# Expert results scattered to token order and read back by plain loads; the first expert's rows prepared in halves

## The chip, the cores and the metric

One core of a Trainium2 chip runs the whole program. The metric is the device time of one execution in microseconds (us). The kernel before takes 1114.15 us, the median of 3 runs (1113.95 to 1116.16).

## The reference, cut to what matters

The program computes two layers of a network over 512 tokens of 1024 numbers each, in float32, and a final RMSNorm. Each layer ends in a mixture of experts (MoE), and the change is there and in what follows it:

```python
def moe_route(flat, router_w, router_b):          # flat: (512, 1024)
    s = sigmoid(flat @ router_w)                  # 16 experts in 4 groups
    biased = s + router_b
    grp_score = sum(top_k(biased per group, 2))   # best group ...
    g_sel = argmax(grp_score)
    idx = top_k(where(in_group, biased, -inf), 2) # ... and the best two experts in it
    w = take(s, idx); w = w / sum(w)
    return combine                                # (512, 16), two weights per token

out = 0
for e in range(16):
    hid = silu(flat @ w_gate[e]) * (flat @ w_up[e])      # 1024 -> 512
    out = out + combine[:, e:e + 1] * (hid @ w_down[e])  # 512 -> 1024
```

After layer 0's MoE comes layer 1's pooling mixer (a norm, four banded averages over neighbouring tokens, four 256x256 products), after layer 1's MoE the final norm. With the reference's inputs the experts get these numbers of tokens: layer 0: 29 46 25 40 87 70 86 61 87 91 82 106 56 62 62 34; layer 1: 31 35 18 26 89 73 76 60 84 87 77 118 51 68 74 57.

## The kernel before

**One expert after the other, 128 rows at a time.** The tokens lie in SBUF as 4 tiles of 128 (`x`). Their normed, modulated rows are also in HBM (`xh_dram`, "xh_scratch" in the profile). From the router's choice DVE and TensorE make, for each expert, a list of its token numbers (`lists`, 128 x 16; places without a token hold 0, so token 0's row is fetched for them). GpSimd fetches an expert's 128 rows with one indirect DMA (`fetch`, L1827) into one of two buffers `xg`. TensorE transposes them (`rows_T`, 8 transposes, L2113), ACT casts the transposed rows to a high part (`rows_high`, L1862), and DVE subtracts it to get a low part (`rows_low`, L2018). The weights stream from HBM through a ring of six half slots of 1 MB in SBUF. ACT makes their high parts (`high`, L1855), DVE their low parts (`low`, L2011). Each product is three matmuls (high x high, high x low, low x high; L2130 for gate and up, L2145 for down).

**A software pipeline.** `step(e)` works on expert e's down product and expert e+1's gate and up products; the steps from 1 on stand in hardware loops. Every engine has its own instruction order, written out by hand, and semaphores tie them. What is done for expert 0 before `step(0)` is written out: TensorE runs `keep_busy` matmuls without use, `rows_T(0)`, more `keep_busy`, waits for the low part of the rows, and then does products 0 and 1 (gate), `rows_T(1)`, products 2 and 3 (up). DVE does `low` of halves 0 and 1, `rows_low(0)`, `low` of halves 2 and 3, `rows_of_tokens` and `weights_of_tokens`, then `step(0)`. SP issues the load of a half slot as soon as `low` has used the previous content.

**Results.** `rows_out` (L2035, the last expert's in two halves on L2077) multiplies an expert's 128 result rows by the layer's gate into one of two buffers `y_sb`. ACT stores all 128 rows to the expert's own place in HBM (`store`, L1875; the last expert's in halves, L1913), `y_dram`, "y_scratch" in the profile. Two buffers mean that a result buffer must be stored before the result two experts later is written.

**The combination.** `rows_of_tokens` computed for every token where its two result rows lie (`row_of`). Once all stores have landed, GpSimd fetches them with 8 indirect DMAs, 2 for each tile of tokens (`fetch` of class `Combine`, L2379), into a buffer of 8 tiles. DVE adds them, weighted: for each tile two instructions `x = rows * weight + x` (L2394). After layer 0, DVE prepares tables of the mixer (L2484 to L2488) before these adds; per tile ACT takes the square sum (L2440), GpSimd makes 1/sqrt of it (L221, L223), ACT normalizes (L2445), TensorE multiplies by the bands (L2515). SP loads the rows of the next norm (L258 to L270) once the tables are done and three tiles are summed. After layer 1, ACT takes the square sum (L2574), GpSimd 1/sqrt, DVE multiplies (L2591) and SP stores the tile (L2567). The weight of the final norm is loaded on L2564.

If an expert has more than 128 tokens, a further slow pass runs; with these inputs none has.

## Time and profile before

| | before |
|---|---|
| median of 3 runs | 1114.15 us |
| the profiled execution's own time | 1112.38 us |
| its span (first to last instruction) | 1110.7 us |
| TensorE busy | 989.0 us, 89% |
| VectorE (DVE) busy | 939.0 us, 85% |
| ScalarE (ACT) busy | 626.4 us, 56% |
| GpSimd (POOL) busy | 104.4 us, 9% |
| DMA traffic | 332.41 MB, 299 GB/s over the span |
| highest GB/s in a fortieth of the span (within the MoE stages) | 413 to 415 |

All times of instructions come from the one profiled execution and count from the start of its span. The span's 1110.7 us and some 1.7 us around it make 1112.38 us, which is 1.8 us under the median of the timed runs. The first 419 us (adaLN rows, attention, layer 0's norm) are not touched by the change. The MoE of layer 0 takes from 419 to 721 us, the mixer and norm of layer 1 to 778 us, the MoE of layer 1 to 1080 us, the final norm the rest.

### The profile page before, as it was taken

What the parts mean: (1) busy time and instruction counts of PE and PEld (TensorE: products, weight loads), DVE (VectorE), ACT (ScalarE), POOL (GpSimd) and SP (SyncE); (2) the same over time, 40 slices, a digit from 0 to 9 for tenths busy, and PEclk for the clock granted to TensorE, in tenths of its full rate; (3) what the DMA queues carried; (4) which work ended last, traced back from release to release, by engine and by line L of the source; (5) the groups of instructions that cost most, each with busy time, mean ns of one, the idle gap of its engine ahead of it and who ended that gap; (6) DMA issues with size and microseconds to landing.
All of it is one profiled execution on the core that took longest, in us unless ns stands there. A gap on an engine that the chain in (4) does not pass through costs nothing. (4 is left out here: it accounts for less than half of the span.)

```text
span 1110.7 us, 14060 instructions
## 1 busy us (share of the span) xinstructions
PE 989.0 (89%) x4898; PEld 802.4 (72%) x4898; DVE 939.0 (85%) x1045; ACT 626.4 (56%) x770; POOL 104.4 (9%) x132
## 2 busy tenths in 40 slices
PE   6689999999798986999999999948799999999980
PEld 1467877777676865788888888737578888888870
DVE  5768988998797858899999999865899999999975
ACT  1635233324676135777777777443477777777741
POOL 0200120000110002000000000042300000000005
PEclk9989999999999998999999999969799999999995
DMA  9726878942301836999999999876599999999946
GB/s 368 286 75 211 280 244 308 323 172 96 151 1 53 309 113 237 345 413 414 415 413 415 413 414 412 296 259 263 205 353 413 413 415 413 414 413 414 414 169 236
DMA packets 148263, 332.41 MB, mean 299 GB/s; under 512 B 16444, under 2 KB 18404, under 8 KB 148088
## 3 DMA queue, kind: packets, MB, share of 16 engines
q1 hardware_dynamic: 127592, 278.72, 65.5%
q10 hardware_dynamic: 13712, 27.92, 7.2%
q0 software_dynamic: 6912, 25.17, 6.0%
q8 instruction: 27, 0.44, 0.2%
q14 instruction: 20, 0.16, 0.0%
HBM read 308.67 MB, written 23.11 MB: 299 GB/s over the span
## 5 line engine op out<-in xcount | busy, mean ns | idle before, releaser
L1855 ACT CAST w_hi<-ring 128x2048 fp32r<-128x2048 f32 x192 | 367.1, 1916 | 112.2 <-PE bank L2130 55.1
L2011 DVE TENSOR_TENSOR w_lo<-ring,w_hi 128x2048 fp32r<-128x2048 f32 x192 | 428.8, 2284 | 1.4 <-POOL mark L1835 1.0
L2130 PE MATMUL bank<-w_hi,xT_hi 128*128 128x512 f32 x512 | 203.4, 397 | 5.2 <-DVE xT_lo L2018 5.2
L2130 PE MATMUL bank<-w_hi,xT_lo 128*128 128x512 f32 x512 | 200.0, 391 | 0.0
L2130 PE MATMUL bank<-w_lo,xT_hi 128*128 128x512 f32 x512 | 199.5, 390 | 0.0
L1511 PE MATMUL bank<-ring_last_parts,arena_parts 128*128 128x512 f32 (+1 forms) x320 | 117.5, 398 | 8.0 <-DVE x_parts L1073 6.5
L2130 PEld LDWEIGHTS bank<-w_hi,xT_hi 128*128 128x128 f32 x512 | 96.1, 188 | 26.1 <-DVE xT_lo L2018 6.9
L2130 PEld LDWEIGHTS bank<-w_hi,xT_lo 128*128 128x128 f32 x512 | 96.2, 188 | 20.8
L2130 PEld LDWEIGHTS bank<-w_lo,xT_hi 128*128 128x128 f32 x512 | 96.3, 188 | 19.1
L1511 PE MATMUL bank<-ring_parts,arena_parts 128*128 128x512 f32 (+1 forms) x256 | 101.0, 395 | 0.0
L1145 DVE SCALAR_TENSOR_TENSOR gate_b<-ring,silu_c,gate_b 128x512 f32<-128x512 f32 x126 | 95.5, 758 | 4.5
L2145 PE MATMUL bank<-w_hi,hT_hi 128*128 128x512 f32 x240 | 93.6, 390 | 0.0
L2145 PE MATMUL bank<-w_lo,hT_hi 128*128 128x512 f32 x240 | 93.5, 389 | 0.0
L2145 PE MATMUL bank<-w_hi,hT_lo 128*128 128x512 f32 x240 | 93.4, 389 | 0.0
L1827 POOL DMA_INDIRECT shared<-xh_scratch,shared x32 | 37.5, 1171 | 428.1 <-PE bank L2113 406.3
L1511 PE MATMUL bank<-ring_last_parts,x_parts 128*128 128x512 f32 x192 | 77.7, 405 | 0.0
L1511 PEld LDWEIGHTS bank<-ring_last_parts,arena_parts 128*128 128x128 f32 x320 | 61.1, 194 | 20.9 <-DVE x_parts L1073 5.8
L1511 PEld LDWEIGHTS bank<-ring_parts,arena_parts 128*128 128x128 f32 x256 | 49.4, 193 | 8.8
L2145 PEld LDWEIGHTS bank<-w_hi,hT_hi 128*128 128x128 f32 x240 | 45.1, 188 | 9.3
L2145 PEld LDWEIGHTS bank<-w_hi,hT_lo 128*128 128x128 f32 x240 | 45.0, 188 | 9.4
L2145 PEld LDWEIGHTS bank<-w_lo,hT_hi 128*128 128x128 f32 x240 | 45.1, 188 | 9.3
L869 ACT ACTIVATE ada_junk<-bank 128x128 f32<-128x128 f32 x80 | 21.0, 278 | 48.0 <-PE bank L1481 25.2
(273 smaller groups left out, 1427.8 us busy)
## 6 DMA issues: line engine op xcount, KB each, us to landing
ring<-in_moe_w_gate SPq DMA_DIRECT2D x64, 1024.0 KB, 9.1
ring<-in_moe_w_down SPq DMA_DIRECT2D x64, 1024.0 KB, 9.6
ring<-in_moe_w_up SPq DMA_DIRECT2D x64, 1024.0 KB, 11.8
ring<-in_ada_w SPq DMA_DIRECT2D x18, 2048.0 KB, 9.1
y_scratch<-shared ACTq DMA_DIRECT2D x30, 512.0 KB, 6.2
ring<-in_w_in ACTq DMA_DIRECT2D x21, 512.0 KB, 4.6
shared<-in_ada_w SPq DMA_DIRECT2D x6, 1024.0 KB, 13.3
x_res<-in_x SPq DMA_DIRECT2D x8, 512.0 KB, 12.1
```

What stands on the lines that cost most here:

```text
L869: last = nc.scalar.activation(ada_junk[:, c * P:(c + 1) * P], bank[:, 7 if i < IN_PROJ else 6 + i - IN_PROJ, c * P:(c + 1) * P], ACT.Ident ...
L1145: ins = nc.vector.scalar_tensor_tensor(ada_acc[:, i % 2, :], w[:, k, :], silu_c[:, 0, k:k + 1], onto, ALU.mult, ALU.add)
L1511: last = pe.matmul(acc(u)[:, c0:c1], hs[h_], ws[w_], start=(kk == 0 and i == 0), stop=(kk == KD - 1 and i == 2))
L1827: pool.indirect_dma_start(out=xg[:, u, :], out_offset=None, in_=xh_dram, in_offset=bass.IndirectOffsetOnAxis(ap=rows, axis=0)).then_inc(s_ ...
L1855: nc.scalar.copy(w_hi[:, buf(u, p), :], half(raw(e, p))).then_inc(s_hi, 3 if isinstance(e, int) and (e, p) == (-1, 3) else 1)
L2011: V.tensor_tensor(w_lo[:, buf(u, p), :], half(raw(e, p)), w_hi[:, buf(u, p), :].bitcast(F32), ALU.subtract).then_inc(s_lo, 3 if isinstance ...
L2130: last = pe.matmul(bank[:, b, :], xs[:, kk, :], ws[:, k, :], start=(kk == 0 and i == 0), stop=(kk == KD - 1 and i == 2))
L2145: last = pe.matmul(bank[:, 6 + hf, :], xs[:, kk, :], ws[:, k, at], start=(kk == 0 and i == 0), stop=(kk == KE - 1 and i == 2))
```

## The change

1. The lists' entries without a token are now 1024 (`NO_ROW`): a table of token numbers minus 1024 is multiplied by the one-hots and 1024 is added as the list is copied. Every indirect DMA gets a bound (`bounds_check`), so rows beyond it are not moved.
2. For every token and each of its two experts a destination in `y_dram` is computed: token number, plus 512 if this expert is the one with the higher number. TensorE makes the destinations' lists with 8 more small matmuls, which stand between `rows_T(1)` and product 2 of the first expert. `row_of` is gone.
3. Results are no longer stored by ACT but by GpSimd: one indirect DMA for each expert (`scatter`) writes its rows to their tokens' places. `y_dram` has 1024 rows.
4. The two weights of a token are swapped where needed, so that weight 0 belongs to the lower expert (5 more small DVE instructions).
5. `Combine.load`: SP reads the 1024 rows with 8 plain loads of 128 rows, into ring slots 2 and 1; the 4 of the lower experts once experts 0 to 14 have been scattered, the 4 of the higher once all have. In layer 1 the load of the final norm's weight now stands behind them on SP. DVE adds the 4 tiles of the lower experts first, then the 4 of the higher. In layer 0, the mixer's tables now come between the two, and the second half of `pool_w` (`gated_weights(1)`) after them; SP's norm loads wait for it.
6. The first expert's rows are transposed, cast and subtracted in two halves of 4 transposes each, `keep_busy(5)` becomes `keep_busy(2)`, and product 0 waits for the first half, product 1 for the second.

```diff
-                for m in range(1, NE):
+                def scatter(e):
+                    pool.wait_ge(s_y, NE + 1 if e == LAST else e + 1)
+                    if e == 0:
+                        pool.wait_ge(s_dests, 1)
+                    pool.indirect_dma_start(out=y_dram,
+                                            out_offset=bass.IndirectOffsetOnAxis(ap=dests[:, e:e + 1], axis=0),
+                                            in_=y_sb[:, e % 2, :], in_offset=None, bounds_check=2 * SEQ - 1,
+                                            oob_is_err=False).then_inc(s_yst[e % 2], 16)
+
+                for m in range(1, NE + 5):
                     u = m % 2
-                    if m >= 2:
-                        pool.wait_ge(s_gt, m - 1)
-                        pool.wait_ge(s_xg[u], 16 * (m // 2))
-                    fetch(u, lists[:, m:m + 1])
+                    if m < NE:
+                        if m >= 2:
+                            pool.wait_ge(s_gt, m - 2) if m > 2 else pool.wait_ge(s_ft, 2)
+                            pool.wait_ge(s_xg[u], 16 * (m // 2))
+                        fetch(u, lists[:, m:m + 1])
+                    if m >= 5:
+                        scatter(m - 5)
...
+                def first_rows_high():
+                    for hf in range(2):
+                        act.wait_ge(s_ft, hf + 1)
+                        nc.scalar.copy(xT_hi[:, 0, hf * KD // 2:(hf + 1) * KD // 2].rearrange("p k t -> p (k t)"),
+                                       bank[:, hf, :]).then_inc(s_fhi, 1)
...
-                def store(e, u):
-                    act.wait_ge(s_y, e + 1)
-                    act.dma_start(y_dram[bass.ds(e * P, P), :], y_sb[:, u, :]).then_inc(s_yst[u], 16)
...
                 def rows_of_tokens():
-                    V.scalar_tensor_tensor(row_tmp[:, 0], e_sel[:], float(P), place[:], ALU.mult, ALU.add)
-                    link(V.tensor_scalar(row_tmp[:, 1], place[:], float(P), None, ALU.is_ge))
-                    for b in range(2, SEQ // P):
-                        link(V.scalar_tensor_tensor(row_tmp[:, 1], place[:], float(b * P), row_tmp[:, 1],
-                                                    ALU.is_ge, ALU.add))
-                    V.scalar_tensor_tensor(row_of[:], row_tmp[:, 1], float((NE - 1) * P), row_tmp[:, 0],
-                                           ALU.mult, ALU.add)
                     V.tensor_reduce(max_count[:], bank[:, 5, NT * NE:(NT + 1) * NE], AX.X, ALU.max).then_inc(s_most, 1)
+                    for c in range(2):
+                        ins = V.tensor_tensor(later[:, c], e_sel[:, c], e_sel[:, 1 - c], ALU.is_gt)
+                    link(ins)
+                    link(V.scalar_tensor_tensor(dest[:], later[:], float(SEQ),
+                                                token_f[:].unsqueeze(1).to_broadcast([P, 2, NT]), ALU.mult, ALU.add))
+                    for c in range(2):
+                        ins = V.tensor_tensor(listed[:, c, :, NE:2 * NE], pick[:, c], cols(dest[:, c], NE), ALU.mult)
+                    ins.then_inc(s_dest, 1)
...
                 keep_busy(6)
-                rows_T(0, 16)
-                keep_busy(5)
-                pe.wait_ge(s_xlo, 1)
+                first_rows_T()
+                keep_busy(2)
+                pe.wait_ge(s_flo, 1)
                 product(2, -1, 0, 0, 0)
+                pe.wait_ge(s_flo, 2)
                 product(2, -1, 0, 1, 0)
                 rows_T(1, 16)
+                pe.wait_ge(s_dest, 1)
+                for c in range(2):
+                    for t in range(NT):
+                        last = pe.matmul(bank[:, DEST_BANK, DEST_AT:DEST_AT + NE], slot_of[:, c, t, :],
+                                         listed[:, c, t, NE:2 * NE], start=(c == 0 and t == 0), stop=(c == 1 and t == NT - 1))
+                last.then_inc(s_in_dests, 1)
                 product(3, -1, 0, 2, 0)
...
-            def fetch(self, pool, most, moe_stored):
-                def tiles(written):
+            def load(self, sp, y_scattered):
+                for c in range(2):
+                    y_scattered(sp, NE - 1 + c)
                     for t in range(NT):
-                        for c in range(2):
-                            pool.indirect_dma_start(
-                                out=self.rows[:, c, t, :], out_offset=None, in_=y_dram[0:written, :],
-                                in_offset=bass.IndirectOffsetOnAxis(ap=row_of[:, c, t:t + 1], axis=0)
-                            ).then_inc(self.loaded[c][t], 16)
+                        at = (c * NT + t) * P
+                        sp.dma_start(self.rows[c][:, t, :], y_dram[at:at + P, :]).then_inc(self.loaded[c][t], 16)
...
             def _(sp):
-                sp.wait_ge(p_wg, 1)
+                combine.load(sp, y_scattered)
+                sp.wait_ge(p_wg, 2)
                 sp.wait_ge(combine.done, NT - 1)
                 front1.load_rows(sp)
...
             def _(dve):
+                for t in range(NT):
+                    combine.add(dve, 0, t)
                 dve.wait_ge(tables, 16 * 8)
...
+                gated_weights(0)
                 for t in range(NT):
-                    combine.add(dve, t)
+                    combine.add(dve, 1, t)
+                gated_weights(1)
...
             def _(sp):
                 y_ready(sp)
+                combine.load(sp, y_scattered)
                 sp.dma_start(fin_w, a["final_norm_w"].partition_broadcast(P)).then_inc(f_ld, 16)
...
             def _(dve):
-                combine.add(dve, 0)
-                combine.add(dve, 1)
+                for t in range(NT):
+                    combine.add(dve, 0, t)
+                combine.add(dve, 1, 0)
+                combine.add(dve, 1, 1)
                 dve.wait_ge(f_ld, 16)
                 for t in range(NT):
                     if t + 2 < NT:
-                        combine.add(dve, t + 2)
+                        combine.add(dve, 1, t + 2)
                     dve.wait_ge(f_rs, t + 1)
```

`rows_out`'s wait for its buffer is on the scatters instead of the stores, two experts earlier.

## Rows read from the trace of the kernel before

**Rows 1.** Busy time by window: us, PE, PEld, DVE, ACT, POOL, PEclk, DMA share, GB/s.

```profile
816.00:833.00 17.00, 17.00 (x81) 14.14 (x80) 16.55 (x10) 12.68 (x9) 0.94 (x1) 1.00 1.03 392
```

**Rows 2.** Timeline, a step of layer 1's MoE: start, duration, instruction, [idle before <-releaser].

```profile
833.83 0.94 POOL L1827 DMA_INDIRECT shared<-xh_scratch,shared  x1 [16.75 <-PE bank L2113]
816.39 6.68 DVE L2011 TENSOR_TENSOR w_lo<-ring,w_hi 128x2048 fp32r<-128x2048 f32 x3
```

**Rows 3.** Chain that ended last, in order of time: start us, us, what.

```profile
786.70 4.24 DMA shared<-xh_scratch,shared
...
1080.24 4.09 DMA y_scratch<-shared
```

**Rows 4.** Timeline of POOL after layer 1's last expert: the last of 8 gathers.

```profile
1094.38 1.02 POOL L2379 DMA_INDIRECT shared<-y_scratch,row_of  x1 [0.30 <-issue]
```

**Rows 5.** Timeline of DVE at the end of layer 1.

```profile
1074.72 1.22 DVE L2035 TENSOR_TENSOR shared<-bank,gate_b 128x1024 f32<-128x1024 f32 x1
...
1091.98 2.60 DVE L2394 SCALAR_TENSOR_TENSOR x_res<-shared,weight,x_res 128x1024 f32<-128x1024 f32 x2 [1.23 <-DMA shared<-y_scratch,row_of]
...
1100.53 2.60 DVE L2394 SCALAR_TENSOR_TENSOR x_res<-shared,weight,x_res 128x1024 f32<-128x1024 f32 x2
...
1106.37 1.28 DVE L2591 SCALAR_TENSOR_TENSOR shared<-x_res,rstd,shared 128x1024 f32<-128x1024 f32 x1 [0.72 <-POOL rstd L223]
```

**Rows 6.** DMA issues: KB each and median us from issue to landing.

```profile
y_scratch<-shared ACTq DMA_DIRECT2D x30, 512.0 KB, 6.2
...
out<-shared SPq DMA_DIRECT2D x4, 512.0 KB, 2.6
...
shared<-in_final_norm_w SPq DMA_DIRECT2D x1, 512.0 KB, 3.9
```

**Rows 7.** Timeline of DVE after layer 0's last expert.

```profile
722.55 2.36 DVE L2488 TENSOR_TENSOR arena<-shared,gate_b 128x1024 f32<-128x1024 f32 x2
...
737.34 3.93 DVE L2394 SCALAR_TENSOR_TENSOR x_res<-arena,weight,x_res 128x1024 f32<-128x1024 f32 x3 [0.26 <-DMA arena<-y_scratch,row_of]
744.28 1.23 DVE L324 SCALAR_TENSOR_TENSOR shared<-shared,arena 128x1024 f32<-128x1024 f32 x1 [3.01 <-DMA arena<-in_norm_ffn_w]
```

**Rows 8.** Timeline of ACT, PE and SP after layer 0's last expert.

```profile
717.97 2.99 ACTq L1913 DMA_DIRECT2D y_scratch<-shared  x2
...
736.77 1.13 ACT L2445 ACTIVATE arena<-x_res,rstd 128x1024 f32<-128x1024 f32 x1
...
737.95 9.64 PE L2515 MATMUL bank<-shared,arena 128*128 128x136 f32 x64 [18.09 <-ACT arena L2445]
...
738.72 0.34 SPq L258 DMA_DIRECT2D shared<-mod_scratch  x1
```

**Rows 9.** Timeline of all engines at the start of layer 1's MoE.

```profile
790.36 2.28 DVE L2011 TENSOR_TENSOR w_lo<-ring,w_hi 128x2048 fp32r<-128x2048 f32 x1
790.71 2.74 POOL L1827 DMA_INDIRECT shared<-xh_scratch,shared  x1 [2.68 <-DVE shared L2054]
790.99 1.92 PE L2113 MATMUL bank<-ident,shared 128*128 128x128 f32 x8 [0.17 <-DMA shared<-xh_scratch,shared]
792.94 1.01 ACT L1862 CAST xT_hi<-bank 128x1024 fp32r<-128x1024 f32 x1 [7.54 <-PE bank L2113]
793.99 1.23 DVE L2018 TENSOR_TENSOR xT_lo<-bank,xT_hi 128x1024 fp32r<-128x1024 f32 x1 [1.35 <-ACT xT_hi L1862]
795.26 0.50 PE L2130 MATMUL bank<-w_hi,xT_hi 128*128 128x512 f32 x1 [1.20 <-DVE xT_lo L2018]
...
815.79 0.68 DVE L2028 TENSOR_TENSOR hT_lo<-bank,hT_hi 128x512 fp32r<-128x512 f32 x1
```

**Rows 10.** Timeline of DVE and PE at the start of layer 0's MoE.

```profile
430.76 2.28 DVE L2011 TENSOR_TENSOR w_lo<-ring,w_hi 128x2048 fp32r<-128x2048 f32 x1
435.08 0.51 PE L2130 MATMUL bank<-w_hi,xT_hi 128*128 128x512 f32 x1 [1.20 <-DVE xT_lo L2018]
...
441.13 1.09 PE L2113 MATMUL bank<-ident,shared 128*128 128x128 f32 x8 [0.27 <-DMA shared<-xh_scratch,shared]
```

195 lines of the change are left out of this document (111 added, 84 removed).

## The prediction

> **What bounds the kernel now.** I read the 40 slices first, then windows over the MoE stages, then the chain of waits around their ends, then timelines of every engine there. In the middle of a MoE, TensorE is busy 17.00 of 17.00 us at full granted clock, with DVE at 16.55, the DMA share at its top and ACT at 12.7 [rows 1]. A step lasts the 16.75 + 0.94 = 17.69 us between two gathers [rows 2]. So 30 steps are TensorE's own time, and neither fewer bytes nor a freer ACT queue can shorten them. Time can change only where TensorE stands: at the start of each MoE and after its last expert. The end of layer 1 shows the price: results ready at 1080.24 [rows 3], the last gather issued at 1094.38 [rows 4], the first tile of x complete at 1091.98 + 1.28 = 1093.26, the last at 1103.13, the last norm's start at 1106.37 [rows 5], the span's end at 1110.7. The reader should see in rows 4 that GpSimd makes 8 gathers one after the other, each 0.94 with 0.30 between, 9.9 us in all.
>
> **The steady steps: 0.** Scatters replace ACT's stores; an expert's 128 rows of 4 KB (0.52 MB) become on average 64, in the gathers as well, so a step moves about 0.52 MB less of 7.3. The cover is TensorE's full row. What is new there: GpSimd now has two indirect DMAs in a step, where it was idle 16.75 us [rows 2]. A gather issued while DVE was inside a `low` took 2.74 instead of 0.94, ending 0.81 after that `low` (790.36 + 2.28 = 792.64; 790.71 + 2.74 = 793.45) [rows 9]. The scatter starts right behind its step's gather, at some 835, when DVE does three `low` in a row (6.68) [rows 2]. From below it costs 0.94, from above it waits for all three: done by about 842 and landed by 849. The next gather is wanted only at 851.5, and the buffer only in the result two steps later, over 30 us on. Both ends give 0. I take 0.
>
> **End of layer 1.** Before: 1080.24 to 1110.7. After, by its links:
> - Expert 14's result is ready at 1074.72 + 1.22 = 1075.94 [rows 5]. The nearest row for a scatter is an uncrowded gather, 4.24 from issue to landing, of which 0.94 is GpSimd's [rows 3, 2]; it lands at 1080.2. The 4 loads of the lower experts go out at 1080.24.
> - A plain 512 KB transfer takes 2.6 (out) to 3.9 (final norm's weight, beside other traffic) [rows 6]. I take 3.0: first tile at 1083.3. Further ones follow at 0.524 MB / 415 GB/s = 1.26 us: 1084.5, 1085.8, 1087.1. Expert 15's scatter shares the engines (57 rows, 0.23 MB, 0.55 us): last one at 1087.6.
> - That scatter is issued at 1080.24; 4.24 and the crowd's 0.5 give 1085.0. The higher experts' loads then stand behind the first four: tiles at 1088.9, 1090.1, 1091.4, 1092.7. Bounds for the scatter: 3.3 (57 rows instead of 128 save 0.7 of transfer, and 0.2 besides) and 6.2, a crowded store to the same memory [rows 6].
> - The final norm's weight, 512 KB, was loaded at 1080.24 and now stands last on SP, behind 8 loads: 1092.7 + 1.3 = 1094.0. This is a wait that the change adds. Behind it on DVE stand the adds of tiles 2 and 3, and all norms.
> - DVE: an add takes 1.28 to 1.30. Lower adds end at 1088.9, tile 0 is complete at 1090.2, tile 1 at 1091.5, wait to 1094.0, tile 2 at 1095.3, norm 0 to 1096.6, tile 3 at 1097.9. From tile 3 complete to the end nothing changes: two norms, square sum, GpSimd's two instructions, last norm, store, before 1110.7 - 1103.13 = 7.57. End at 1105.4.
> - Gain 5.3. If the weight arrives in time, tile 3 is complete 1.2 sooner (1/sqrt is then the limit): 6.5. With the scatter at 6.2, all is 1.2 to 1.5 later: 3.9. Were all waits at their lower ends, 8.
>
> **End of layer 0.** Results are ready at about 720.6, the second of ACT's last stores (717.97 + 2.99 less its issue of 0.34) [rows 8]. By the same links the lower tiles land at 723.4 to 727.7, and their adds end at 729.0. Now come the mixer's tables, which stood in an idle stretch before: they ended at 722.55 + 2.36 = 724.91 [rows 7] after starting near 721.1, 3.8 us, of which one `pool_w` half (1.15) is moved on: 2.7. So 731.7; the higher tiles are there by then (from 729.0). x tiles complete at 733.0, 734.3, 735.6, 736.9; before, the last was at 737.34 + 3.93 = 741.27 [rows 7]. But ACT does two square sums before its first normalization, of 1.15 each: 735.5, then 1.13: TensorE starts the bands at 736.65 instead of 737.95. Its 64 matmuls ran 9.64 without a gap [rows 8], so they end 1.3 sooner, not 4.4. DVE's last half of `pool_w` ends at 738.1, and SP's norm loads go out then instead of at 738.72 [rows 8]; with the same 5.5 to landing the scale that they feed (744.28) [rows 7] starts 0.6 sooner, ends at 744.9 and frees DVE in time for the first pooled bank, due at 746.36 - 1.3 = 745.1. Gain 1.3. Lower bound -1.3 (scatters at 6.2 put the lower tiles 2 us later, and with them all else), upper bound 3.
>
> **Starts of the MoEs.** Layer 1: rows landed at 790.94, 8 transposes took 1.92 (half clock), cast 1.01, subtraction 1.23, first product at 795.26 [rows 9]. After: 4 transposes 0.96, half cast 0.6, half subtraction 0.68 (as the same size at 815.79) [rows 9]. DVE is in `low` until 792.6, so the half subtraction can begin at 790.36 + 2.20 = 792.56 and end at 793.24: first product at 793.3, 1.95 sooner. The second half's cast (to 793.5) and subtraction (to 794.1) are needed at 796.1. Two `keep_busy` at half clock (0.87) end at 793.7 if they all run after the transposes: 1.6 instead of 1.95. Layer 0: 430.76 + 2.20 + 0.68 = 433.64 against 435.08: 1.4 [rows 10]. The first gather now moves 29 and 31 rows instead of 128, about 0.9 us less, but `keep_busy(6)` holds TensorE until about its old landing: 0.
>
> What the lead meets next: `rows_T(1)`, which waited 0.27 for its gather at 441.13 [rows 10]. That gather was issued beside a `low` and shared the engines; with 46 or 35 rows in place of 128 I expect it 2 us earlier, so the wait goes. Then the destinations: DVE finishes two `low` (4.4) after the second half subtraction, at 798.5 in layer 1, and needs some 0.85 for six small instructions of 0.17 spaced 0.1 to 0.2: 799.35. TensorE ends `rows_T(1)` at 793.3 + 5.45 + 0.87 = 799.6: the wait is covered with 0.3 to spare. If the cover is gone it costs that difference. The 8 small matmuls cost about 0.3. DVE's small instructions grow by some 0.7 in all, in an idle stretch of over 3 us before `rows_low(1)`. Net: layer 1 1.95 - 0.3 = 1.65, less if `keep_busy` holds; layer 0 1.4 + 0.27 - 0.3 = 1.4. Together 3.0, bounds 0 and 3.6.
>
> **Sum.** 5.3 + 1.3 + 3.0 = 9.6. Against the profiled execution's 1112.38 (span 1110.7) that is 1102.8; that execution lay 1.8 below the median of 1114.15, and against the median it is 1104.5.
>
> **Rivals.**
> 1. *Scatters land late.* The destination is HBM, and the stores to it took 6.2 in the crowd [rows 6]. Against it: the last, uncrowded store took 4.09 [rows 3]. Layer 1 gives 3.9, layer 0 -1.3, starts 3.0: 5.6, 1108.5. The Trainium skill ("Perfetto Trace Analysis", "DMA Instruction — HWDGE (DVE, Sync)") says that the semaphore waits for the write to be confirmed, and that this can be surprisingly long where the target is HBM. By that rule this rival is the forecast; of the trace, the 4.09 speaks against it and the 6.2 does not decide, since those stores ran beside a full weight stream. No scatter is in the trace.
> 2. *The starts give nothing*: the second gather lands as late as before (rows 10's wait), or the destinations come late and hold TensorE. 6.6 gained: 1107.5.
> 3. *Faster links*: loads do not queue as full transfers, the weight is there in time. 6.5 + 2 + 3.0 = 11.5 to 13: 1102.
> 4. *Slower than before: bounded indirect DMAs are dear.* Four of them stand on the path, the first gather and the last scatter of each layer. Each takes GpSimd 0.94 now; with a check for each row and a write address computed for each it might take 5. The gain is used up at 9.6 / 4 = 2.4 more each; at 4 more each it is 16 - 9.6 = 6.5 slower, 1120.6. For it: nothing here is bounded or scatters. Against it: all plain gathers lie within 0.94 to 1.4 outside a `low`.
> 5. *The parts cancel or the skipped rows are not skipped, with small losses*: within 0.2%.
>
> **How the numbers follow.** Forecast 0.52; rival 1 0.16; rival 2 0.09; rival 3 0.14; rival 4 0.06; rival 5 0.03. The likeliest is 1104.5. The range 1100 to 1109.5 takes in rivals 1 to 3 and leaves out 4, 5 and the far ends of the others. A measurement here can tell about 0.2% (2.2 us). Faster 0.91, same 0.03, slower 0.06.
>
> **What would show it.** Right: 17.69 us steps with fewer GB/s; the last scatter lands 4 to 5 after 1080.2, tile 3 complete 5 sooner, the final norm's weight as what DVE waits for after tile 1; bands some 1.3 sooner though the last x tile is 4 sooner; first products 1.4 and 1.95 sooner and `rows_T(1)` without a wait. Wrong: scatters over 6 us, a gather or scatter of several us on GpSimd, a step longer than 17.69, or TensorE waiting for the destinations.

## The result: 0.7% slower, where 0.9% faster was forecast

The changed kernel takes 1122.88 us, the median of 4 runs (1122.12 to 1123.76), against 1115.09 of the kernel before on the same chip (4 runs, 1113.95 to 1116.16): ratio 1.0070, interval 1.0053 to 1.0088. A second measurement on another chip gave 1.0059, 1.0044 to 1.0074. The profiled execution has a span of 1120.4 us against 1110.7. Forecast were 1104.5 (1100 to 1109.5).

The page of the changed kernel (busy time with share of the span; then 40 slices; then DMA issues, KB each and median us to landing):

```profile
PE 991.3 (88%) x4908; PEld 801.8 (72%) x4908; DVE 940.0 (84%) x1057; ACT 625.7 (56%) x772; POOL 192.7 (17%) x148
...
GB/s 353 295 76 223 277 241 254 337 191 74 171 1 27 309 120 210 305 384 374 384 389 387 375 375 387 296 258 260 153 307 391 373 381 388 386 376 379 386 187 228
...
ring<-y_scratch SPq DMA_DIRECT2D x16, 512.0 KB, 5.5
```

GpSimd is busy 88 us more, and the MoE slices move 373 to 391 GB/s instead of 412 to 415; less traffic was forecast. Unforeseen is the first slice: 353 GB/s, where the kernel before moved 368, in code that the change does not touch.

The steady step of layer 1, timeline of POOL, then of DVE (they answer to [rows 2]):

```profile
843.65 2.77 POOL L1833 DMA_INDIRECT shared<-xh_scratch,shared  x1 [14.79 <-PE bank L2150]
846.72 1.92 POOL L1850 DMA_INDIRECT y_scratch<-shared  x1 [0.30 <-issue]
861.33 2.80 POOL L1833 DMA_INDIRECT shared<-xh_scratch,shared  x1 [12.69 <-PE bank L2150]
```

```profile
843.27 6.68 DVE L2036 TENSOR_TENSOR w_lo<-ring,w_hi 128x2048 fp32r<-128x2048 f32 x3
```

The gather now begins 0.38 us inside a `low` and takes 2.77 instead of 0.94 (before, it began 0.11 ahead of one, at 851.52 against 851.63), the scatter 1.92; a step is 861.33 - 843.65 = 17.68 us, as before.

The start of layer 1's MoE, PE (answers to [rows 9]; the last line is `rows_T(1)`):

```profile
800.37 1.97 PE L2157 MATMUL bank<-ident,shared 128*128 128x128 f32 x8
...
803.40 0.50 PE L2175 MATMUL bank<-w_hi,xT_hi 128*128 128x512 f32 x1 [0.55 <-DVE xT_lo L2043]
...
809.82 1.10 PE L2150 MATMUL bank<-ident,shared 128*128 128x128 f32 x8 [0.69 <-DMA shared<-xh_scratch,shared]
```

The two indirect DMAs ahead of it on POOL, and the mark and first `low` that the first releases:

```profile
796.66 1.38 POOL L1833 DMA_INDIRECT shared<-xh_scratch,shared  x1 [8.68 <-DVE shared L1993]
798.04 0.09 POOL L1842 MEMSET mark<- 1x1 f32 x1
801.35 2.27 POOL L1833 DMA_INDIRECT shared<-xh_scratch,shared  x1 [3.22 <-DVE shared L2087]
```

```profile
795.67 0.16 DVE L1993 TENSOR_SCALAR shared<-bank 128x1 uint32<-128x1 f32 x1
...
798.16 2.29 DVE L2036 TENSOR_TENSOR w_lo<-ring,w_hi 128x2048 fp32r<-128x2048 f32 x1 [1.13 <-POOL mark L1842]
```

From the first list's index (795.67) to the first `low` it is 2.49 us; before it was 1.80. The second gather, 35 rows, lands 8.4 us after 801.35, and TensorE waits 0.69 for it. The 128 rows of before took longer, 9.9 us, but they were asked for earlier: 12.61 us after the first cast of this MoE (778.10) instead of 13.83 (787.52).

The end of layer 1: the chain of waits, then DVE (they answer to [rows 3] and [rows 5]):

```profile
1090.23 8.42 DMA y_scratch<-shared
...
1100.52 8.27 DMA shared<-in_final_norm_w
```

```profile
1088.77 0.69 DVE L2114 TENSOR_TENSOR shared<-bank,gate_b 128x512 f32<-128x512 f32 x1 [1.96 <-PE bank L2230]
1093.07 2.58 DVE L2453 SCALAR_TENSOR_TENSOR x_res<-ring,weight,x_res 128x1024 f32<-128x1024 f32 x2 [3.61 <-DMA ring<-y_scratch]
1096.54 1.28 DVE L2453 SCALAR_TENSOR_TENSOR x_res<-ring,weight,x_res 128x1024 f32<-128x1024 f32 x1 [0.88 <-DMA ring<-y_scratch]
1098.85 1.29 DVE L2453 SCALAR_TENSOR_TENSOR x_res<-ring,weight,x_res 128x1024 f32<-128x1024 f32 x1 [1.03 <-DMA ring<-y_scratch]
1102.39 2.53 DVE L2453 SCALAR_TENSOR_TENSOR x_res<-ring,weight,x_res 128x1024 f32<-128x1024 f32 x2 [2.25 <-DMA ring<-y_scratch]
1108.81 1.28 DVE L2453 SCALAR_TENSOR_TENSOR x_res<-ring,weight,x_res 128x1024 f32<-128x1024 f32 x1 [3.88 <-DMA shared<-in_final_norm_w]
```

The scatter lands 8.42 us after its issue (forecast 4.7), while the four loads of the lower halves, issued from 1089.48, run beside it. The new wait for the final norm's weight is where the prediction put it, but 3.88 long.

The end of layer 0, from DVE, POOL and PE (they answer to [rows 7] and [rows 8]):

```profile
725.78 0.69 DVE L2114 TENSOR_TENSOR shared<-bank,gate_b 128x512 f32<-128x512 f32 x1 [1.98 <-PE bank L2230]
730.86 1.28 DVE L2453 SCALAR_TENSOR_TENSOR x_res<-ring,weight,x_res 128x1024 f32<-128x1024 f32 x1 [4.39 <-DMA ring<-y_scratch]
...
739.56 4.86 DVE L2453 SCALAR_TENSOR_TENSOR x_res<-ring,weight,x_res 128x1024 f32<-128x1024 f32 x4
```

```profile
742.11 1.16 POOL L220 TENSOR_SCALAR rstd<-stats 128x1 f32<-128x1 f32 x1 [13.89 <-ACT arena L2498]
743.36 2.63 POOL L222 TENSOR_TENSOR rstd<-rstd,minus_half 128x1 f32<-128x1 f32 x1
```

```profile
747.23 4.98 PE L2576 MATMUL bank<-shared,arena 128*128 128x136 f32 x24 [21.48 <-ACT arena L2503]
```

Results are ready at 726.47, the last x tile is complete at 744.42: 17.95 us, against 20.7 before and 16.3 forecast. But the bands start at 747.23, 20.8 us after the results, against 17.35 before (720.6 to 737.95). A second profile of the same kernel (after_again) shows 17.6 there, with these rows of GpSimd:

```profile
743.23 0.19 POOL L220 TENSOR_SCALAR rstd<-stats 128x1 f32<-128x1 f32 x1 [13.67 <-ACT arena L2498]
743.51 0.57 POOL L222 TENSOR_TENSOR rstd<-rstd,minus_half 128x1 f32<-128x1 f32 x1
```

So 3 us of this stretch come and go between executions. Above, DVE makes the last four additions in one row (4.86 us) and 1/sqrt takes 1.16 + 2.63; in after_again DVE waits 0.35 us for a row tile after two of them, 1/sqrt starts in that gap and takes 0.19 + 0.57. Of the other profiles, ring_only, y_large, whole_first and scatter_alone look like the first; ring_lower, pad32_y_large, spread, unbounded and both of moved like the second; pad32, with 0.19 + 1.45, lies between.

### The profile page after: what moved, and what is told of

Its sections match the earlier page's. It is cut to its first block and busy times, and to the rows that moved or that the text cites. A ratio compares the mean times of both kernels' runs of the same rounds, so it can differ in the third digit from the quotient of the medians.

```text
span 1120.4 us, 14018 instructions
## 1 busy us (share of the span) xinstructions
PE 991.3 (88%) x4908; PEld 801.8 (72%) x4908; DVE 940.0 (84%) x1057; ACT 625.7 (56%) x772; POOL 192.7 (17%) x148
## 5 line engine op out<-in xcount | busy, mean ns | idle before, releaser
L1833 POOL DMA_INDIRECT shared<-xh_scratch,shared x32 | 76.9, 2402 | 344.7 <-PE bank L2150 294.8
L2175 PEld LDWEIGHTS bank<-w_hi,xT_lo 128*128 128x128 f32 x512 | 96.1, 188 | 20.8
L1850 POOL DMA_INDIRECT y_scratch<-shared x32 | 66.2, 2068 | 119.5 <-DVE shared L2068 106.5
## 6 DMA issues: line engine op xcount, KB each, us to landing
ring<-in_moe_w_up SPq DMA_DIRECT2D x64, 1024.0 KB, 12.8
x_res<-in_x SPq DMA_DIRECT2D x8, 512.0 KB, 12.6
```

Of the source, the lines that this page charges most:

```text
L1833: pool.indirect_dma_start(out=xg[:, u, :], out_offset=None, in_=xh_dram, in_offset=bass.IndirectOffsetOnAxis(ap=rows, axis=0), bounds_chec ...
L1850: pool.indirect_dma_start(out=y_dram, out_offset=bass.IndirectOffsetOnAxis(ap=dests[:, e:e + 1], axis=0), in_=y_sb[:, e % 2, :], in_offset ...
L2175: last = pe.matmul(bank[:, b, :], xs[:, kk, :], ws[:, k, :], start=(kk == 0 and i == 0), stop=(kk == KD - 1 and i == 2))
```

## The experiments

Each was timed beside the kernel before; ratios are to it, with their 95% interval. Runs of one kernel spread over some 6 us, and the slower ones are mostly those with the lower mean granted clock: in moved_again the five runs up to 1112.9 us had 0.962 to 0.967, the six from 1114.9 us on 0.953 to 0.959. Which of the two causes the other is not shown. In the profiles of the changed kernel's versions with an aligned ring the untouched first stage ended anywhere between 420.5 and 425.4 us. So single profiles are compared link by link, and from the first cast of layer 0's MoE to the end. "pad" means this edit, which puts the ring and all behind it at the addresses of the kernel before:

```diff
+        sb("row_pad", [P, 8])
         max_count = sb("max_count", [P, 1], I32)
         ring_parts = parts_of("ring_parts", 3 * SLOT_W)
         ring = sb("ring", [P, 3, SLOT_W])
```

| kernel | ring at byte | time | ratio | MoE 0 to end, profile |
|---|---|---|---|---|
| before | 42752 | 1115.6 to 1117.3 | 1 | 691.8 |
| changed, again (profiles of both) | 42720 | 1122.83 | 1.0059 (1.0044 to 1.0074) | 696.7, 692.6 |
| pad32 | 42752 | 1117.59 | 1.0005 (0.9989 to 1.0022) | 693.4 |
| before_shifted | 42784 | 1126.43 | 1.0098 (1.0072 to 1.0123) | 701.9 |
| before_shifted_64 | 42816 | 1126.62 | 1.0093 (1.0072 to 1.0115) | 699.5 |
| before_shifted_128 | 42880 | 1124.95 | 1.0077 (1.0061 to 1.0094) | 701.8 |
| ring_only | 42720 | 1123.62 | 1.0062 (1.0047 to 1.0077) | 697.1 |
| ring_lower | 42496 | 1117.54 | 1.0016 (1.0005 to 1.0027) | 690.9 |
| y_large | 42720 | 1122.26 | 1.0046 (1.0028 to 1.0064) | 697.8 |
| pad32_y_large | 42752 | 1117.11 | 1.0018 (1.0004 to 1.0032) | 691.8 |
| spread | 42752 | 1118.97 | 1.0017 (1.0002 to 1.0032) | 692.1 |
| unbounded | 42752 | 1117.85 | 1.0020 (1.0004 to 1.0036) | 690.7 |
| whole_first | 42752 | 1120.57 | 1.0027 (1.0011 to 1.0043) | 696.2 |
| before_halves | 42752 | 1115.47 | 0.9993 (0.9979 to 1.0007) | 692.3 |
| scatter_alone | 42752 | 1124.02 | 1.0055 (1.0037 to 1.0073) | 697.6 |
| scatter_first | 42752 | 1116.08 | 1.0006 (0.9992 to 1.0020) | 691.7 |
| best | 42752 | 1116.31 | 1.0009 (0.9995 to 1.0023) | 692.5 |
| moved | 42752 | 1115.29 | 0.9978 (0.9963 to 0.9993) | 690.4 |
| moved_again | 42752 | 1114.88 | 0.9989 (0.9976 to 1.0001) | 688.6 |

### Where the loss comes from: the ring's address

**pad32**, the changed kernel with the pad.

> The changed kernel with 32 unused bytes per partition in the place of the removed row_of, so that the weight ring and everything allocated behind it lie at the addresses of the kernel before (42752 instead of 42720 bytes into the partition). Theory A (addresses: the shift by 32 bytes takes the buffers off multiples of 64 and slows every DMA into them): the first stage ends 4 to 5 us sooner, the first 20 us move 350 GB/s again, and the whole falls from 1122.9 to 1110 to 1116 us. Theory B (the new indirect DMAs and waits alone cost the time, the first stage's 4.8 us are drift of the chip): 1121 to 1124 us, no change.

**before_shifted**, the kernel before with the same line, which there shifts the ring off its place.

> The kernel before with 32 unused bytes per partition added ahead of the ring (42784 instead of 42752), nothing else. Theory A (addresses): slower by 8 us or more, since a steady step already needs 414 GB/s and the slowed DMA can't give that: 1122 to 1140 us, with TensorE waiting in the steady steps. Theory B: 1114 to 1116 us as before.

Windows of each, columns as in [rows 1]; first the kernel before, then the changed one, pad32, before_shifted:

```profile
2.00:20.00 18.00, 11.39 (x22) 2.28 (x23) 11.31 (x19) 1.50 (x2) 0.00 (x0) 1.00 1.03 388
600.00:617.70 17.70, 17.70 (x86) 14.80 (x85) 16.78 (x11) 13.30 (x9) 0.94 (x1) 1.00 1.04 414
```

```profile
2.00:20.00 18.00, 11.23 (x22) 2.23 (x23) 11.03 (x19) 1.50 (x2) 0.00 (x0) 1.00 1.03 373
600.00:617.70 17.70, 17.70 (x86) 14.80 (x85) 16.76 (x10) 12.52 (x9) 5.03 (x2) 1.00 1.03 380
```

```profile
2.00:20.00 18.00, 11.20 (x24) 2.24 (x25) 11.19 (x19) 1.50 (x2) 0.00 (x0) 1.00 1.03 387
```

```profile
2.00:20.00 18.00, 11.00 (x21) 2.12 (x22) 10.86 (x18) 1.50 (x2) 0.00 (x0) 1.00 1.03 371
600.00:617.70 17.70, 17.27 (x83) 14.02 (x82) 16.20 (x11) 12.63 (x10) 1.51 (x1) 1.00 1.04 398
```

The DMA share is full in every row, and the same transfers run at 388 and 387 GB/s with the aligned ring, at 373 and 371 with the shifted one: 4% less. Unchanged code lost 10 us by 32 bytes. There the loss reaches the steady MoE, which wants 414 GB/s and gets 398: TensorE works 17.27 of 17.70 us. Its two MoEs take 4.0 and 3.0 us longer from the first cast to the last results. The changed kernel wants only some 385 and keeps its steps, so it loses less: by its two measurements (1.0070 and 1.0059 against 1.0005) pad32 is 6 to 7 us faster, with an uncertainty of 2.5. Its 1117.6 us lie above the 1110 to 1116 expected, and it is the lowest ratio of the changed kernel's versions with an aligned ring: ring_lower and pad32_y_large, below, have 1.0016 and 1.0018. All of them against all with the shifted ring (1.0046 to 1.0070) make it about 5 us.

The profiles tell roughly where these lie. I compare the means of four with the shifted ring (the changed kernel twice, ring_only, y_large) and five with an aligned one and the same order at the ends (pad32, pad32_y_large, ring_lower, spread, unbounded). The first stage ends 2.8 us later, the bands of layer 0 start 2.9 us later after the results, the end of layer 1 is 1.0 longer, and the MoEs differ by less than 0.8. The 2.9 are mostly the longer 1/sqrt, in full in three of the four and in none of the five (pad32 has half of it); that a later first row tile closes DVE's gap is argued, not tested.

**before_shifted_64, before_shifted_128, ring_lower**: which multiple is needed. The first two make the pad 16 and 32 words; ring_lower is the changed kernel with seven small tiles moved behind the ring:

```diff
-        norm_a = sb("norm_a", [P, 2, KD])
...
+        sb("ring_pad", [P, 8])
+        ring_parts = parts_of("ring_parts", 3 * SLOT_W)
+        ring = sb("ring", [P, 3, SLOT_W])
+        norm_a = sb("norm_a", [P, 2, KD])
...
-        ring_parts = parts_of("ring_parts", 3 * SLOT_W)
-        ring = sb("ring", [P, 3, SLOT_W])
```

> The kernel before with 64 unused bytes per partition ahead of the ring instead of 32 (before_shifted, 10 us slower, had 32). The ring and all behind it then start at byte 42816 of a partition, a multiple of 64 and not of 128; in before it is 42752, a multiple of 256, in before_shifted and in the changed kernel a multiple of 32 only. Theory Q (what matters is a multiple of 64): the first stage's transfers run at 387 to 388 GB/s again in the window from 2 to 20 us, the time is that of before, 1115.6 to 1117. Rival R (it takes a multiple of 128 or 256): 372 GB/s and about 1126.

> The kernel before with 128 unused bytes per partition ahead of the ring (32 and 64 both cost 10 us). The ring starts at 42880, a multiple of 128 and not of 256. Theory S (a multiple of 128 is enough): 387 to 388 GB/s in the window from 2 to 20 us and the time of before, 1115.5 to 1117.5. Rival T (a multiple of 256 is needed, or this one address): 372 GB/s, 1126.

> The changed kernel with some small tiles moved from ahead of the ring to behind it, so that the ring starts at 42496, 256 bytes below its place in before and pad32, again a multiple of 256; what lies behind it stands as in pad32. Theory W (any multiple of 256 does it): the time of pad32, 1117 to 1118.5, ratio 1.000 to 1.002. Rival X (only the one address 42752 is good, or something else than the multiple): the time of the changed kernel, 1122 to 1123.

Both shifts cost as much as 32 bytes, against what I had expected of 64; the second address that is a multiple of 256 is as good as the first. The window of before_shifted_128:

```profile
2.00:20.00 18.00, 10.97 (x22) 2.18 (x23) 11.07 (x19) 1.50 (x2) 0.00 (x0) 1.00 1.04 372
```

**ring_only**, the changed kernel with the pad behind the ring.

> The changed kernel with the 32 unused bytes behind the ring instead of ahead of it: the ring alone starts at 42720 as in the changed kernel, all behind it (shared memory, the weights' high and low parts, the transposed rows) stands where it stands in before and in pad32. Theory U (it is the place that the weights' transfers write to): 373 GB/s from 2 to 20 us, the time of the changed kernel, 1122 to 1123. Rival V (engines that read and write the high and low parts at such places are slower and disturb the transfers): 387 GB/s and the time of pad32, 1117.6.

```profile
2.00:20.00 18.00, 11.29 (x24) 2.29 (x25) 11.09 (x19) 1.50 (x2) 0.00 (x0) 1.00 1.03 388
40.00:45.00 5.00, 4.32 (x12) 2.82 (x11) 2.54 (x6) 3.78 (x7) 0.00 (x0) 0.50 1.04 389
```

Its time is that of the changed kernel, yet its window from 2 to 20 us is at full rate, against my expectation of 373. Of the 8 MB issued for that window, 6 go to the shared memory behind the ring. From 40 to 45 us only loads into the ring run; there it moves 389 GB/s, as the changed kernel (388), where pad32 moves 403:

```profile
40.00:45.00 5.00, 4.32 (x12) 2.88 (x11) 2.50 (x5) 3.78 (x7) 0.00 (x0) 0.50 1.05 403
```

So two statements hold: the rate follows the address that a transfer writes, and the kernel's time follows that of the ring. The engines' own use of the high and low parts (rival V) plays no role.

**after_again**:

> The changed kernel as it is, in as many rounds as the others, for a narrower interval beside them: 1122.9 had an interval of 1.0053 to 1.0088. By the address alone (pad32 at 1.0005) all of it should be the shift: 1.005 to 1.008 again.

1.0059, as expected.

**y_large** and **pad32_y_large** give `y_dram` its former 8192 rows, of which 1024 are used, in the changed kernel and in pad32.

> The changed kernel with y_scratch kept at its former size of 8192 rows in HBM, of which 1024 are used; SBUF addresses as in the changed kernel. Theory A (SBUF addresses): 1122 to 1124 us. Rival E (the smaller HBM tensor moves other tensors to places where their reads are slower): 1113 to 1118 us and a first stage as fast as before.

> pad32 with y_scratch as large as in before (32 MB, of which 4 MB are used). All eight profiles of the changed kernel with an aligned ring are 2.2 to 5.8 us behind before at 175 us into the span, in code that the change does not touch, where engines wait for weights to land; two profiles of before and before_halves are not. If the place of other buffers in HBM does it, it is as in before here: MoE of layer 0 starts at 419 to 420, time 1114.5. If it does not (y_large against the changed kernel showed nothing, 1122.3 against 1122.9): 421.5 to 425 and 1117.5.

Neither differs from its partner: the layout in HBM is not it. The first stage ended later in all profiles of the changed kernel with an aligned ring (420.5 to 425.4) than in those of before and before_halves (418.9, 419.1). The latter two are of executions that lie 3.8 and 2.4 us under the medians of their kernels (1116.2 and 1115.5), so part of the difference is the choice of execution. The granted clock goes along with it: of the eleven changed kernels with an aligned ring, the five with 0.91 in the window from 40 to 60 us end this stage at 420.5 to 422.1 us, the six with 0.74 to 0.77 at 421.6 to 425.4. What delays the landings there stays open.

### The starts of the MoEs

**spread** (pad32 with the lists' places dealt out so that the rows of a short list spread over the partitions):

```diff
-        "k_places": np.arange(P, dtype=np.float32)[None, :],
+        "k_places": ((np.arange(P) % 8) * 16 + np.arange(P) // 8).astype(np.float32)[None, :],
```

> As the padded kernel, and the list's places are permuted: place s lies in partition (s mod 8 groups reversed: partition p holds place (p mod 8)*16 + p/8), so that an expert's rows are spread over all groups of 8 partitions instead of filling the first ones. Theory C (each of the 16 DMA engines carries 8 neighbouring partitions, so a short list left the first engines with as much as a full one): gathers and scatters land sooner, in the median 1 to 2 us, the second gather by 2 us or more, TensorE's wait for it goes, and the whole is 2 to 4 us faster than the padded kernel. Rival D (landing is set by the crowd and by GpSimd's issue, not by rows per engine): within 0.5 us of the padded kernel.

The gathers landed in 9.0 us in the median, against 9.2, and the time is the same within the noise. The rows' places do not matter here.

**unbounded** (pad32; both list copies end in `ALU.add, ALU.min` with 511, and `fetch` has no bound):

> pad32 with gathers that are not bounded: empty places read row 511 instead of being skipped, so each gather moves 128 rows again; the scatters stay bounded. Theory M (the bound costs GpSimd's queue time): from the first list's index to the first subtraction of a weight part it is 2.0 us as before, not 2.6, so the first product starts 0.6 to 0.7 sooner in each MoE; the second gather lands as in the kernel before or up to 1 us later, since it moves 0.5 MB instead of 0.15, and the steady steps stay at 17.7 with some 14 GB/s more. Time 1117.5, between 1116.5 and 1118.5. Rival N (the bound costs nothing, the later start is an accident of code loading or of the scatter behind it): 2.6 us again. If skipped rows shorten a gather in the crowd, rows_T(1) waits 1 to 2 us longer than in pad32, and the time is 2 to 3 us worse.

Index to first `low`: 1.96 and 1.83 us in the two layers instead of 2.63 and 2.49, so the bound costs 0.66. The second gather with 128 rows was transposed no later (22.3 us after the first cast in both layers; pad32 22.6 and 22.8). Here two things cancel. From its start this gather took 10.0 and 9.6 us to land, where the bounded ones of pad32, with 46 and 35 rows, took 8.6 and 9.0; but it started at 12.3 and 12.6 us after the first cast instead of 14.0 and 13.8. All profiles agree: 8.8 to 10.4 us for 128 rows, from a start at 12.1 to 12.8, and 7.7 to 9.1 for a bounded gather, from 13.3 to 14.0. So with the skipped rows the landing is 1 to 2 us shorter (0.5 of it on GpSimd, 2.27 against 2.74), and the later start takes this back. The first gather is alike: 3.5 to 3.8 us instead of 4.2 to 4.8. In layer 1 TensorE now waited 1.39 for it instead. Time unchanged.

The steady step shows the bound once more. POOL in unbounded, with the `low` beside it:

```profile
854.73 0.97 POOL L1834 DMA_INDIRECT shared<-xh_scratch,shared  x1 [14.40 <-PE bank L2150]
```

```profile
854.84 4.49 DVE L2036 TENSOR_TENSOR w_lo<-ring,w_hi 128x2048 fp32r<-128x2048 f32 x2
```

The unbounded gather begins 0.11 us ahead of the `low`, takes 0.97 and lands in 6.6 us in the median of all; the bounded one begins inside it, takes 2.8 and lands in 9.2 (pad32). It costs no time, as the step has room for both.

**whole_first** (pad32 with the first rows whole and `keep_busy(5)`) and **before_halves** (the kernel before with the halves alone):

> pad32 with the first expert's rows transposed, cast and subtracted whole, behind which TensorE has five waiting products instead of two, as in the kernel before. Theory J (the second gather takes the gain back): the first product starts 1.3 to 1.9 us later than in pad32, but the transposes of the second expert's rows then find these landed, where pad32 waits 0.95 and 1.20 for them; each MoE is 0.3 to 1 us longer, the time 1118.2 to 1119.5. Rival K (the halves are worth their full price): 1.4 and 1.95, 1121. Rival L (nothing at all): 1117.6.

> The kernel before with the halves alone: first expert's rows transposed, cast and subtracted in two halves, two waiting products in place of five behind them; whole gathers, ACT's stores and the indirect gathers at the end as they were. Undoing the halves in pad32 cost 3.0 us by the medians (interval of the two ratios' difference about 2.6 either way), though in the profiles the first subtraction of the second expert's rows stood 0.4 later in one layer and 0.6 sooner in the other. Theory J (the second gather's landing takes the gain back): first products 1.4 and 1.95 sooner, rows_T(1) waits for its gather, 0 to 1 us gained in all: 1115.3 to 1116.2. Rival K (full price): 3 us gained, 1113.

PE at the start of layer 1's MoE in before_halves; the first line is the first expert's transposes, the last `rows_T(1)`:

```profile
791.93 1.97 PE L2136 MATMUL bank<-ident,shared 128*128 128x128 f32 x8 [0.41 <-DMA shared<-xh_scratch,shared]
...
801.65 1.10 PE L2129 MATMUL bank<-ident,shared 128*128 128x128 f32 x8 [1.47 <-DMA shared<-xh_scratch,shared]
```

The first product stood 1.1 and 1.5 us earlier than before, `rows_T(1)` 0.1 later in both layers (22.36 and 22.84 us after the first cast, against 22.26 and 22.75). Time 0.9993: theory J. whole_first had no wait before `rows_T(1)`, which also stood where pad32 had it, within 0.6. Its profile is 2.8 us longer than that of pad32 from the first cast to the end. Of these, 2.1 are the bands' later start after layer 0's results, with the long 1/sqrt (1.17 + 2.63) that comes and goes between executions. So the profile shows no price of the halves. Whether the 3 us between the medians have the same source is not shown; the two intervals overlap.

### The ends of the layers

**moved** (on pad32):

```diff
+                    if c and between:
+                        between()          # layer 1: the load of the final norm's weight
                     y_scattered(sp, NE - 1 + c)
...
-                for t in range(NT):
-                    combine.add(dve, 0, t)
                 dve.wait_ge(tables, 16 * 8)
...
                 gated_weights(0)
+                for t in range(NT):
+                    combine.add(dve, 0, t)
```

> The padded changed kernel (pad32: span 1118.1, time 1117.6) with two things reordered. In layer 1 the final norm's weight is loaded between the lower and the higher half of the result rows, while SP waits for the last scatter; in layer 0 DVE prepares the mixer's tables ahead of the lower rows' additions, in the 3.56 us in which it waits for the first of them, instead of behind them. Theory F (order): both are waits of order alone. The 3.04 us in which DVE waited for the weight go, and the additions of the higher tiles in layer 0 start about 2.5 us sooner (737.1 instead of 739.7), so the mixer's first square sum with them: 5 us off the time of pad32, 1112.5, and 3 to 4 better than the kernel before. Rival G (crowd): the result rows' own traffic sets these times. The weight's 0.5 MB then delays the scatter and the higher rows behind it by what it saves, and in layer 0 the first higher rows land no sooner than 739: 1 us or nothing, 1116.5 to 1117.5.

DVE at its end, columns as in [rows 5]:

```profile
1096.27 2.49 DVE L2456 SCALAR_TENSOR_TENSOR x_res<-ring,weight,x_res 128x1024 f32<-128x1024 f32 x2 [2.29 <-DMA ring<-y_scratch]
1098.94 1.28 DVE L2456 SCALAR_TENSOR_TENSOR x_res<-ring,weight,x_res 128x1024 f32<-128x1024 f32 x1 [0.17 <-DMA ring<-y_scratch]
```

The wait for the weight is gone; from results ready (1083.13) to the last x tile it is 20.0 us, to the end 28.8, where pad32 took 30.0 and before 30.5. Of the 5 us expected 2 to 3 came (0.9978 and, below, 0.9989, against pad32's 1.0005); the rest met 1/sqrt on GpSimd and the higher rows' landing. In layer 0 the bands started 17.5 us after the results, where pad32 took 18.3; but the other aligned profiles with the old order, whole_first and scatter_alone apart, took 16.8 to 17.4, so a gain there is not shown. **moved_again** was to show whether this beats the kernel before:

> The kernel moved once more on another chip and with other runs of before beside it (0.9978, interval 0.9963 to 0.9993). If its gain over before is real: 0.9965 to 0.999 again; if it was the luck of one chip: 1.000 or above.

0.9989 there, 0.9978 the first time: 0.1 to 0.2% faster, about the size that can just be told; the second interval reaches 1.0001.

**scatter_alone** (pad32, `y_scattered(sp, NE)` for both halves) and **scatter_first** (moved; SP also waits until GpSimd has issued the last scatter):

```diff
+                nc.gpsimd.memset(mark[:], 0.0).then_inc(s_last_out, 1)   # behind scatter(LAST)
...
             def y_scattered(eng, experts):
+                eng.wait_ge(s_last_out, 1)
```

> pad32 with the loads of the lower halves held back until all scatters have landed, so that the last scatter of each layer runs with nothing beside it (in pad32 four 512 KB loads run beside it, and it landed 8.33 us after its issue in layer 1). Theory H (the crowd): the scatter lands 3.5 to 4.5 after its issue, as an uncrowded gather of before. The 8 loads then come in one row behind it. In layer 1 the last higher tile lands at about 1088.86 + 4.2 + 2.5 + 8 x 1.26 = 1105.6 against some 1101.5 in pad32, so the time is 2 to 4 us worse in each layer: 1121 to 1125. Rival I (a scatter to HBM is slow by itself, as the page rule on writes says): it lands after about 8 again, and the time is 6 to 9 worse in each layer, 1130 or more.

> The kernel moved (1115.3, span 1111.9) with one more wait: SP starts the loads of the lower halves only when GpSimd has issued the last scatter, some 1.7 us later than now (1083.16 to about 1084.9 in layer 1). In moved that scatter was issued at 1083.91 and landed at 1092.57, together with the last of the four loads that were issued 0.75 us ahead of it. Theory O (transfers are served in the order in which they were issued): with the scatter first it lands 4 us after its issue, at 1088, while the lower loads land 1.7 later than now; the higher loads then follow directly, their last lands some 3 us sooner, and both layers gain: 3 us in layer 1, 1 to 3 in layer 0, time 1110 to 1112. Rival P (the queues share the engines packet by packet, and each packet in the crowd is slow): it lands after 8 us again, and each layer loses the 1.7 us: 1118 to 1119.

POOL and SP at the end of layer 1 in moved:

```profile
1083.91 0.97 POOL L1851 DMA_INDIRECT y_scratch<-shared  x1 [3.30 <-DVE shared L2115]
```

```profile
1083.16 1.77 SPq L2448 DMA_DIRECT2D ring<-y_scratch  x4
...
1092.57 1.75 SPq L2448 DMA_DIRECT2D ring<-y_scratch  x4
```

The same in scatter_first:

```profile
1085.79 0.97 POOL L1852 DMA_INDIRECT y_scratch<-shared  x1 [3.30 <-DVE shared L2117]
```

```profile
1086.92 2.11 SPq L2451 DMA_DIRECT2D ring<-y_scratch  x4
...
1089.62 2.39 SPq L2451 DMA_DIRECT2D ring<-y_scratch  x4
```

SP's second group goes out when the scatter has landed: 8.66 us after the scatter's issue in moved, 3.83 in scatter_first, and 3.8 in scatter_alone. So a bounded scatter to HBM is not slow by itself; it lands with the loads that were issued 0.75 us ahead of it. The Trainium skill ("Perfetto Trace Analysis", "DMA Instruction — HWDGE (DVE, Sync)") says that waiting for the write's confirmation can cause a long delay where the target is HBM; 3.8 us shows none of weight. The Trainium skill also says ("DMA: Bandwidth & Descriptors", "Queues, rings and completion order") that each engine serves its queues in turn, packet by packet; by that the 57 rows would be let in between the loads. The DMA view of moved, from 1084 to 1088 us and from 1089 to 1090 (packets, MB, share of 16 engines; the scatter is in q0):

```profile
q1 hardware_dynamic: 328, 1.21, 93.2%
```

```profile
q1 hardware_dynamic: 80, 0.28, 70.4%
q0 software_dynamic: 69, 0.11, 28.5%
```

Order of issue and taking turns each hold in part: up to 1088, for the first 4 us after its issue, nothing of the scatter moved, and then the two queues shared the engines. In scatter_first its packets ran from 1087 on, 1.2 us after the issue. What held them back in moved is not shown.

But the early scatter gained nothing (1.0006, where 1110 to 1112 us were expected of theory O and 1118 to 1119 of rival P): the last x tile was complete 20.1 us after the results, as in moved (20.0). In moved the DMA engines ran from 1084 with a gap from 1092 to 1094 (131 GB/s); scatter_first has no such gap, but starts its loads 1.9 us after the results (31 GB/s from 1084 to 1086, 80 from 1086 to 1088), and moves 4.8 MB from 1088 to 1102. So I take it, without a test of its own, that the 4.9 MB of this stretch set it. A window of scatter_first:

```profile
1096.00:1098.00 2.00, 0.00 (x0) 0.00 (x0) 0.55 (x1) 0.00 (x0) 0.00 (x0) 0.50 1.01 393
```

**best** (scatter_first with unbounded gathers):

> scatter_first with the gathers not bounded (empty places read row 511), whose first products came 0.7 us sooner but whose time was that of pad32. If the second gather's landing sets the start: the time of scatter_first within 1 us, 1110 to 1112 by theory O, 1118 to 1119 by rival P. If the bound's 0.7 us twice were worth its price: 1.3 less than scatter_first.

1.0009: no more than its parts. The lowest ratio is that of moved.

## Why the prediction was wrong

- **Bound of the steady step, 0: right.** 17.68 us, less traffic, two indirect DMAs of 2.8 and 1.9 on GpSimd without cost. The gather's 2.8 was not foreseen: the bound makes it start inside a `low`.
- **The step that failed first is one that the prediction does not have.** Its sum adds the two ends and the starts and puts everything else at nothing. It has no term for the place of the buffers in SBUF and gives no reason for leaving it out. But `row_of`'s 32 bytes stood ahead of the ring. Worth +5 to 7 us: pad32 against the changed kernel, and before_shifted against before for the cause.
- **End of layer 1, 5.3 forecast.** Tile 3 complete was to be 17.7 us after the results; it was 23.0 in the changed kernel and 20.0 in moved. Two terms failed. The scatter's "4.24 and the crowd's 0.5" was 8.4, since it stood behind four loads; rival 1 had the place, with 6.2, but its reason (HBM) was wrong. And "further ones follow at 1.26" was 2.3 for the fourth lower tile (1096.54 to 1098.85). The forecast wait for the norm's weight was real and 3.9 long (3.0 in pad32) instead of 2.5. From the results to the end the changed kernel lost 0.5 against before (30.9 and 30.5), pad32 gained 0.5, and the two profiles of moved, which takes the wait away, 1.7 and 2.1.
- **End of layer 0, 1.3 forecast.** The x tiles did come 2.7 us sooner after the results (4.4 forecast), but the first of them was complete at 740.84, 14.4 us after the results instead of 12.4, and then the link through GpSimd was longer: 1.16 + 2.63 for 1/sqrt where moved, whose additions have gaps, shows 0.19 + 0.57. After the results, the bands started 3.4 us later than before in one profile of the changed kernel, 0.3 later in the other and 0.9 later in pad32; in the other four aligned profiles of the same order they started between 0.6 sooner and at the same time. So without the long 1/sqrt this end gave about 0. A small slip besides: by the links of layer 1 the lower tiles land at 723.7 to 728.0, not 723.4 to 727.7.
- **Starts, 3.0 forecast: 0.** Rival 2, for both of its reasons but one. First products came 1.3 us sooner in layer 1 and 0.2 sooner in layer 0 instead of 1.95 and 1.4, as the bounded gather delays the first `low` by 0.7. Then `rows_T(1)` waited for its gather. "I expect it 2 us earlier" is the sentence that failed, and not for its price of the bytes: from start to landing the bounded gather was 1.3 and 1.5 us shorter (8.7 and 8.4 instead of 10.0 and 9.9). What the prediction left out is its start, 1.7 and 1.2 us later after the first cast. In layer 1 this is the bound's doing: it holds back the first gather, the `low` behind it and, by 0.5, the second gather. before_halves has the halves without the bound and gained no more: its gather landed as in before, and `rows_T(1)` waited 1.5 us. The destinations' wait was covered, as forecast.
- **Rival 4** (bounded indirect DMAs dear) had the right sign and a small core: 0.7 us at the first gather, not 4, and 1.2 by the start of the second.
- The sum without the address: pad32 at 1.0005, ring_lower at 1.0016, pad32_y_large at 1.0018, so 9.6 us of forecast gain became a loss of 0.5 to 2 us, with 1 to 2 us of uncertainty each.

## What to carry to other kernels

Note the SBUF address of every large DMA target before and after a change, and keep it at a multiple of 256 bytes: here a removed 32-byte tile cost more than all else in the change gave. Price a transfer in a full DMA stream by what was issued ahead of it as well as by its bytes and by when it starts, and put small loads that are needed last into the wait before the big ones. If work is pulled forward at the start of a pipeline, look for the next thing that lands late before counting the gain. Before a stage's difference between two kernels is explained, look whether two profiles of one kernel differ as much.

## What the runs showed of the hardware

- Transfers to SBUF addresses that are multiples of only 32, 64 or 128 bytes ran at 370 to 373 GB/s, those to multiples of 256 at 387 to 389, at a full DMA share in both cases. Transfers of 512 KB to 2 MB over 128 partitions; other shapes were not tried.
- A bound on an indirect DMA costs about 0.66 us on GpSimd. With the entries that it skips (46 and 35 rows instead of 128) the second gather of a MoE landed 7.7 to 9.1 us after its start instead of 8.8 to 10.4. A bounded scatter of 57 rows with no load ahead of it landed in 3.8 us.
- GpSimd's indirect DMA takes 2.8 us instead of 0.94 when it begins inside a 2.28 us subtraction on DVE, and its 128x1 power took 2.63 instead of 0.57 beside DVE's uninterrupted additions; where DVE paused for 0.35 us or more as it began, it took 0.57.
